# Two attention heads of a pair in one burst, on the two column halves of TensorE

## The reference

```python
proj = h @ w_in                        # 3*512 attention, 4*512 mLSTM, 16 gate columns
aq, ak, av, mq, mk, mv, mo, mg = jnp.split(proj, cuts, axis=-1)
aq = partial_rotary(split_heads(aq, 8), positions) * 64 ** -0.5
ak = partial_rotary(split_heads(ak, 8), positions)
attn_out = merge_heads(dilated_attention_mixture(aq, ak, split_heads(av, 8)))
...                                    # mlstm_out from mq, mk, mv, mo, mg, both directions
merged = jnp.concatenate([attn_out, mlstm_out], axis=-1)
return merged @ w_out
```

## Time and profile before

| | us |
|---|---|
| three timed runs | 2228.42, 2233.67, 2236.56 (median 2233.67) |
| the profiled execution | 2231.22 (span of its instructions 2229.2) |
| TensorE matmuls busy | 2161.7 (97%) |
| TensorE weight loads busy (beside the matmuls) | 1820.5 (82%) |
| VectorE busy | 1282.5 (58%) |
| ScalarE busy | 1021.2 (46%) |
| L965, the products of the change | 64 records, 15.1 busy |

### The profile page before, as it was taken

One profiled execution on the slowest core, in us unless ns is written; L12 is line 12 of the kernel. 1 busy time (PEld: TensorE's weight loads), 2 busy tenths in 40 slices (PEclk: granted clock), 3 DMA queues, 4 the chain that ended last, 5 costly groups with the idle time before them and its releaser, 6 DMA issues.

```text
span 2229.2 us, 26907 instructions
## 1 busy us (share of the span) xinstructions
PE 2161.7 (97%) x11220; PEld 1820.5 (82%) x11220; DVE 1282.5 (58%) x1400; ACT 1021.2 (46%) x1166; POOL 106.2 (5%) x234
## 2 busy tenths in 40 slices
PE   7999989999999999999999999999999999999998
PEld 7878867888978889888878888878888888877887
DVE  5655555455565555755565457775556455877543
ACT  4454444444454444454444444654445444555442
POOL 0010011000010000000020000010001000001000
PEclk9999989999999999999999999999999999999999
DMA  8475546555445556465565554236557555424552
GB/s 258 152 258 186 189 151 191 180 187 191 146 150 190 189 169 198 163 208 189 187 224 189 189 163 140 95 127 199 186 168 252 182 186 173 130 91 153 185 185 94
DMA packets 291512, 392.46 MB, mean 176 GB/s; under 512 B 10356, under 2 KB 257956, under 8 KB 291264
## 3 DMA queue, kind: packets, MB, share of 16 engines
q1 hardware_dynamic: 283744, 368.22, 51.0%
q10 hardware_dynamic: 4032, 14.68, 2.1%
q0 software_dynamic: 3616, 7.85, 1.2%
HBM read 389.65 MB, written 2.11 MB: 176 GB/s over the span
## 4 chain that ended last, share of the span: by engine, by line
PE 87%; DVE 6%; ACT 3%; DMA 2%; issue 1%; POOL 1%; ACTq 0%; SPq 0%; POOLq 0%; DVEq 0%
PE psum L516 27%; PE psum L518 26%; PE psum L517 26%; DVE w_lo L1392 3%; PE psum L574 2%; ACT w_hi L1048 1%; ACT squares L1074 1%; PE psum L603 1%; DMA raw<-in_ffn_w_in 1%; PE psum L937 1%; PE psum L965 1%; DVE X L1834 0%; POOL rstd L1875 0%; DMA raw<-in_ffn_w_up 0%; DMA raw<-in_conv_w_in 0%
## 5 line engine op out<-in xcount | busy, mean ns | idle before, releaser
L1392 DVE TENSOR_TENSOR w_lo<-raw,w_hi 128x2048 fp32r<-128x2048 f32 x349 | 797.5, 2290 | 467.4 <-ACT w_hi L1048 467.0
L1048 ACT ACTIVATE w_hi<-raw 128x2048 fp32r<-128x2048 f32 x349 | 664.7, 1911 | 274.3 <-PE psum L518 187.9
L516 PE MATMUL psum<-w_hi,xT 128*128 128x512 f32 (+1 forms) x1840 | 698.0, 379 | 21.3 <-DVE xT L1427 10.8
L517 PE MATMUL psum<-w_lo,xT 128*128 128x512 f32 (+1 forms) x1840 | 685.0, 372 | 0.0
L518 PE MATMUL psum<-w_hi,xT 128*128 128x512 f32 (+1 forms) x1840 | 684.7, 372 | 0.0
L516 PEld LDWEIGHTS psum<-w_hi,xT 128*128 128x128 f32 x1840 | 348.6, 189 | 88.9 <-issue 19.2
L518 PEld LDWEIGHTS psum<-w_hi,xT 128*128 128x128 f32 x1840 | 348.6, 189 | 62.0
L517 PEld LDWEIGHTS psum<-w_lo,xT 128*128 128x128 f32 x1840 | 349.4, 190 | 57.6
L516 PE MATMUL psum<-w_hi,h_hi 128*128 128x512 f32 x768 | 306.8, 399 | 8.1 <-DVE h_lo L1434 4.4
L518 PE MATMUL psum<-w_hi,h_lo 128*128 128x512 f32 x768 | 303.7, 395 | 0.0
L517 PE MATMUL psum<-w_lo,h_hi 128*128 128x512 f32 x768 | 303.5, 395 | 0.0
(11 more groups left out here) (214 smaller groups left out, 1380.5 us busy)
## 6 DMA issues: line engine op xcount, KB each, us to landing
raw<-in_ffn_w_in SPq DMA_DIRECT2D x176, 512.0 KB, 4.8
raw<-in_ffn_w_gate SPq DMA_DIRECT2D x88, 512.0 KB, 4.0
raw<-in_ffn_w_up SPq DMA_DIRECT2D x88, 512.0 KB, 5.0
raw<-in_ffn_w_down SPq DMA_DIRECT2D x44, 1024.0 KB, 4.9
raw<-in_ffn_w_out SPq DMA_DIRECT2D x44, 1024.0 KB, 4.9
raw<-in_mix_w_in SPq DMA_DIRECT2D x28, 1024.0 KB, 5.3
raw<-in_conv_w_in SPq DMA_DIRECT2D x24, 1024.0 KB, 5.2
raw<-in_attn_w_qkv SPq DMA_DIRECT2D x12, 1024.0 KB, 5.3
```

Of the source, the lines that this page charges most:

```text
L516: pe.matmul(dst, l_hi, r_hi, start=first, stop=False, skip_group_check=loose)
L517: pe.matmul(dst, l_hi, r_lo, start=False, stop=False, skip_group_check=loose)
L1048: return act.activation(dst, source, ACT.Copy, **kw)
L1392: dve.tensor_tensor(w_lo[u % LO_RING][:], raw[u % LO_RING][:], f32(w_hi[hi_slot[u]][:]), ALU.subtract).then_inc(lo_ready, 1)
```

## The change

`head_out(hd)` becomes `two_heads_out(j)`: heads 2j and 2j+1 are multiplied in one place, and the loop over k (two blocks of 128 keys) is outside the loop over the two heads, so that the instructions alternate between the two column halves of the array. It raises pv_done once per pair, and ScalarE waits for one increment where it waited for two. The places between the halves of units 7, 9 and 11 become empty.

```diff
-                def head_out(hd):
-                    pe.wait_ge(at_ready, b_at + hd + 1)
-                    if hd in (2, 4):
-                        pe.wait_ge(head_ready, b_head + hd // 2)
-                    if hd == 4:
+                def two_heads_out(j):
+                    pe.wait_ge(at_ready, b_at + 2 * j + 2)
+                    if j in (1, 2):
+                        pe.wait_ge(head_ready, b_head + j)
+                    if j == 2:
                         pe.wait_ge(in_read, b_in + 11)
-                    elif hd == 6:
+                    elif j == 3:
                         pe.wait_ge(in_read, b_in + 14)
-                    r0 = 64 * (hd % 2)
                     for k in range(2):
-                        mm = pe.matmul(psum[r0:r0 + 64, 2 if hd < 6 else 5, 0:S], av[:, k, hd * 64:(hd + 1) * 64],
-                                       a_probT[hd % 2][:, k, :], start=k == 0, stop=k == 1)
+                        for e in range(2):
+                            hd = 2 * j + e
+                            mm = pe.matmul(psum[64 * e:64 * e + 64, 2 if j < 3 else 5, 0:S],
+                                           av[:, k, hd * 64:(hd + 1) * 64], a_probT[e][:, k, :],
+                                           start=k == 0, stop=k == 1, skip_group_check=True)
                     mm.then_inc(pv_done, 1)
...
-                    if 7 <= n < 13:
-                        head_out(n - 7)
+                    if n in (8, 10, 12):
+                        two_heads_out((n - 8) // 2)
...
-                head_out(6)
-                head_out(7)
+                two_heads_out(3)
...
-                        act.wait_ge(pv_done, seen.next(pv_done, 2))
+                        act.wait_ge(pv_done, seen.next(pv_done))
```

## The result

Timed beside the kernel before, 22 runs each: **2235.69 us** (2230.34 to 2240.66) against 2232.48 us (2228.42 to 2236.56), ratio 1.0015, 95% interval 1.0008 to 1.0021. So the change buys nothing: it costs 3.2 us in the first group and 0 in the second, where 2.5 us of gain were forecast. (One run of the change in h1, 4327 us, about twice as long as all others, is left out.)

A forecast was written before the change was run, and what follows sets the result against it. TensorE was taken to bound the kernel (87% of the last chain), with VectorE nearly full in units 7 to 9. Of 7.1 us saved, 4.6 become waits: 2232.5 - 2.5 = 2230.0 us, range 2223.5 to 2236.0.

The forecast's parts named there:

- A lone burst: One head's four passes standing alone in a mixer unit, put at 1.20 us of TensorE; two adjacent heads at 1.22 us.
- gain at the transposes of unit 7: Head 0 leaves unit 7: TensorE 0.72 us earlier, 0.48 us lost as a new wait for VectorE's a_prob.
- of unit 8: At unit 8's transposes, with the first pair (+0.02 us) there, TensorE is 0.69 us earlier.
- of unit 9: At unit 9's transposes the gain stays 0.69 us; the head's whole 1.20 us becomes a wait for a_prob.
- gain per layer at head 7: After units 11 and 12 and heads 6 and 7, each mixer layer gains 1.24 us.
- the wait for it that I had left at 0.52 us: TensorE's existing wait in unit 10 for VectorE's Y, forecast to stay 0.52 us as both arrive earlier.
- can come or go with a shift of the whole program: 1.3 us of clock loss at the w_out units after the xT waits, said to move single executions only.
- 4.6 us of new waits: Of 7.1 us saved on TensorE in both layers, 4.6 us turn into waits for VectorE in units 7, 9, 11.
- the head start is given back: Rival: something behind the mixers is late on its own clock, weights or granted clock; 2232.5 us, chance 0.14.
- One after the other: Rival: alternating column halves run in turn, 0.92 us more for each of four pairs; 2234.9 us, chance 0.06.
- program order: Rival: passes leave in program order, 0.22 us more per pair, gain 0.80 per layer; 2230.9 us, chance 0.10.
- All of it comes back: Rival: VectorE's waits are shorter because its operations start earlier with TensorE's; 2225.4 us, chance 0.10.

The follow-up runs named there:

- h1: The same changed kernel run once more beside the kernel before, in another group on one chip (11 runs against 31); ratio to before 1.0000.
- f2: The changed kernel with the two loops swapped, so both matmuls of the even head come before those of the odd one; ratio to before 1.0009.
- f1: The changed kernel with four unread products ahead of unit 7's transposes and nine ahead of unit 9's, in the new waits; ratio to before 0.9997.
- g1: The changed kernel with unread products in units 7 and 9, plus 19 in the old wait for xT before the w_out units; ratio to before 0.9987.
- h2: The changed kernel with two of five taps of the mixer's convolution left out on VectorE, so not computing the reference; ratio to before 0.9968.
- its control: The kernel before with two of five taps of the mixer's convolution left out on VectorE; ratio to before 1.0001.
- h4: The kernel before with the products of heads 0 and 2 left out, so units 7 and 9 have no burst; ratio to before 1.0022.

## Why the prediction went wrong

*Right.* A lone burst costs 1.20 us and a pair nothing more (1387.19 to 1388.64 less two steps of 0.12 is 1.21 us); the alternation does nothing. Wait by wait the forecast holds where the clock does (second layer):

| step | forecast | measured |
|---|---|---|
| gain at the transposes of unit 7 | 0.72 | 0.73 |
| of unit 8 | 0.69 | 0.67 |
| of unit 9 | 0.69 | 0.79 |
| gain per layer at head 7 | 1.24 | 1.49 |
| both layers, by the schedule alone | 2.5 | 3.0 |

The 0.25 us missing came from unit 10: Y was nearer, and the wait for it that I had left at 0.52 us shrank to 0.29 in the second layer:

```profile
1963.59 0.61 DVE L1692 TENSOR_SCALAR Y<-psum,den_inv 128x128 f32<-128x128 f32 x2
...
1964.35 0.35 PE L921 MATMUL psum<-v_ext,wmat 128*128 128x130 f32 x1 [0.29 <-DVE Y L1692]
```

*Wrong.* The time lies inside the stated 2223.5 to 2236.0 us, by 0.3 us, but the change moved the other way than forecast. The step that failed is the one on the clock: that a fall "can come or go with a shift of the whole program", and "moves single executions, not the forecast". I had the pieces in hand: a fall of 1.3 us behind a wait in the second layer, and 4.6 us of new waits that I had just computed myself. I priced those waits as time that comes back as nothing. On TensorE they cost more than nothing: the mean clock is 0.0020 lower (h1, f2), of which one fall of 6.8 us per execution makes 0.0015. That is nominally 4.5 us, or 3.4 us at the 2.56 of 3.4 that one fall was seen to cost. Against 3.0 us of gain this makes +0.4 us; h1 measured 1.0000, f2 1.0009, the first group 1.0015. The 0.5% that the prediction took for the least difference that can be told was too coarse as well: 22 runs of each told 0.15%.

*The rivals.* The rival "the head start is given back" (2232.5 us) had the size of h1 and was 3 us under the first group; it named weights and the clock of the stages behind, not the waits of the change itself. "One after the other" named the nearest time, 2234.9 us, by luck: it and "program order" fell with the 1.08 us bursts. "All of it comes back" fell with the 0.92 us wait.

*Open.* The account of +0.4 us rests on one fall's 2.56 of 3.4 us. Over all runs of each kernel the time is 1.2 us shorter where the clock is 0.001 higher, which would make the 0.0020 only 2.5 us, less than the 3.0 us of gain. The falls at the start of the second mixer are not placed either. It is open why the first group stands 1.5 thousandths above before and h1's group does not: the change ran at 0.9886 there and 0.9897 in h1, worth 2.5 us nominally, and the clock of before in the first group isn't listed. Nor is it shown what decides in which layer the clock falls; the two layers do the same work, and one fell in each of the four traces. So that the waits cost clock is shown; that they account for the whole difference is not.

## What to carry to other kernels

Taking work off TensorE ahead of a wait for another engine turns it into idle time, and idle time among small products can cost clock behind it: price it at something, and look at the granted clock in windows, not at the wait alone. Cheap unread products in the wait kept the clock here (f1, g1); only g1, which fills an older wait too, came out faster than before, by 0.13%. A shorter list on the other engine was worth more (h2, 7 us against its control), but h2 got it by leaving work out, which a real kernel can't. Before pairing products for the sake of overlap, look for a place where they already stand together: it gives the price of a pair for nothing.

## What the runs showed of the hardware

- Two products of 64 columns on the two column halves run side by side whether their instructions alternate or stand one after the other: eight passes in 1.08 to 1.09 us, four in 1.08. The Trainium skill says in "TensorEngine Tiling (Array Packing)", Key Properties, that tiles work independently and that only a change of tiling mode drains the array; the trace agrees with the first, and no run here singles out the second.
- In 4 of 8 layers the granted clock fell to 1.2 GHz for 6.8 us right behind a stretch such as the 3.70 us in which TensorE was busy 2.77 or 2.78 us, with one wait of 0.9 us in it (the change's second layer, busy 2.79, had no fall), and in none of 6 layers with the wait filled. The Trainium skill tells in "TensorE: Matmul & The Clock Gate", HAM oscillation, of a clock lost to waits for DMA between bursts; here the clock fell behind a wait of 0.9 us for VectorE, in half of the layers that had it.
- Leaving out work (h4) made the kernel slower by 0.22%.
